# Attention probabilities normalised before their transposition, instead of the output after it

## The chip, the cores and the metric

The kernel runs on one core of a Trainium2 chip. The metric is device time in microseconds (us) of one execution. The core has five engines that run their own instruction streams and meet only at semaphores: TensorE (PE; its weight loads are listed apart as PEld), VectorE (DVE), ScalarE (ACT), GpSimd (POOL) and SyncE (SP), which here only starts transfers.

## What is computed

Two transformer-like layers on 1024 tokens of width 1024 in float32. The change touches only the two attentions of the second layer. Of the reference that is:

```python
# dilated_window_attention: three patterns, each softmax(q k^T / 8 + bias) v, merged by their
# denominators: one softmax over all positions, with a bias table per head
p = jnp.exp(s - m)
den = jnp.sum(p, axis=-1)
o = jnp.einsum('bnrhqk,bnkrhd->bnqrhd', p, vw) / den_q[..., None]
...
# latent_attention, per block of 128 queries
s = jnp.where((qpos[:, None] >= kpos[None, :])[None, None], s, -jnp.inf)
p = jax.nn.softmax(s, axis=-1)
return jnp.einsum('bhqk,bkhd->bqhd', p, v)
...
mixed = jnp.concatenate([o_a * jax.nn.silu(z_a), o_b * jax.nn.silu(z_b)], axis=-1)
```

So each attention output is divided by the sum of its exponentials and multiplied by a gate (`z_a`, `z_b`).

## The kernel before

The first layer and the projections of the second are large matrix products on PE. The attentions come late: stage A (the dilated one) fills about 2042 to 2177 us of the span, stage B (the latent one) about 2230 to 2387 us, with the latent projections in between.

Each stage has 32 **units**. A unit is a pair of heads (`j`, 0 to 3) and a block of 128 queries (`qb`); `at_unit(u)` takes the blocks of a pair in the order 0, 7, 1, 6, 2, 5, 3, 4. I call them positions 0 to 7 of a pair. A unit with block `qb` sees w = 128 (qb + 1) keys, so its width goes 128, 1024, 256, 896, 384, 768, 512, 640, and eight units make one period of the pattern. Its steps:

- `z(u)` on PE: scores of both heads into the PSUM tile `sm`, of which there is one.
- `scores(u, hh)` on DVE (L2918 in the profile): adds the bias or mask, writes `att_s` in SBUF (four places, by unit) and the row extremum.
- `exps(u, hh)` on ACT (L2269): exponential in place, with the row sum in `small`.
- `roots(u)` on DVE (L2926): the reciprocal of the two sums, 128x2.
- `turn(u)` on PE (L1693): 2 (qb + 1) transpositions of 128x128 out of `att_s`, four to a PSUM bank. Such a group of four is a chunk. Three banks are used in turn, so a chunk waits until the third chunk before it has been copied out.
- The chunks are copied to `att_pt` in SBUF, those with an even number by ACT (L2281), the odd ones by DVE (L2939).
- `output(u)` on PE: first two products that spread the inverse sums over the 64 columns of each head (L1703, into `at_share_place()`), then the probabilities times `v` (L1709, into `at_o_place()`). Both places are single, so `output(u)` waits for `at_o_taken` of unit u - 1.
- Gating on DVE: gate times output (L2951), then times the spread inverse sums (L2953), which raises `at_o_taken`.

The order on each engine is written out by hand. PE runs, unit after unit, `turn(u)`, `z(u+3)`, `output(u)`. DVE runs the odd copies of u, `scores(u+3, 0)`, `roots(u+2)`, `scores(u+3, 1)`, then the gating of u. ACT runs an even copy of u, `exps(u+2, 0)`, the other even copies, `exps(u+2, 1)`. Each stage begins with `z` and `scores` of units 0 to 2, the exponentials of units 0 and 1 and `roots` of units 0 and 1. Line numbers such as L1693 are those of this kernel.

POOL does little here. In stage A it splits late weights once (L878, L880, about 2078 to 2085 us), at the start of stage B again, and in stage B, whenever a pair of heads is finished (`at_o_taken` has reached a multiple of eight), it splits the gated tiles into a high and a low part (`split_mix`, L1083 and L1085).

Of the kernel before, what the change touches and what calls it, by code (L numbers as in the profile page):

```python
# [8 lines left out]
P = 128  # L9
# [3 lines left out]
HALF = 512  # L13
# [3 lines left out]
C = 64  # L17
# [18 lines left out]
ALU = mybir.AluOpType  # L36
# [112 lines left out]
def merge_adds(q):  # L149
# [18 lines left out]
    "rk_post1", "rk_chain", "rk_local", "rk_state", "rk_y", "rk_y_sb", "rk_yc", "rk_yc_sb", "rk_yc_sq", "rk_var",  # L168
    "rk_var_ln", "rk_rstd", "rk_g", "rk_y_done",
    "g_split", "h_split", "bias_p", "n2_sq", "n2_ss", "n2_q", "at_z", "at_o_taken", "at_o",  # L170
    "at_p", "at_pt", "at_root", "at_half_gated", "rot", "sines",
    "hn_sq", "hn_ss", "rot_used", "rope_mid", "hn_rt", "mix_high", "c_high",
    "out_t", "w_high", "root", "high", "x_turned", "tok_root", "x_scaled", "sc_done", "sg_var", "sg_root",
    "sb_e", "sb_p", "c_first", "silu", "g_raw", "g_high", "angles", "x_normed", "p_free0", "p_free1",
# [18 lines left out]
def hybrid_layers(nc, x, mix_norm_g, w_in, gate_b, sc_conv_w, sc_out, sb_out, rw_mu, rw_w0, rw_w2,  # L193
# [10 lines left out]
    with ExitStack() as ctx:  # L204
# [12 lines left out]
        ident = fixed("ident", [P, P])  # L217
# [190 lines left out]
        gp = ctx.enter_context(nc.psum_tensor("gp", [P, 2, T], F32))  # L408
# [171 lines left out]
        def at_unit(u):  # L580

            return u // 8 % 4, BLOCK_ORDER[u % 8]

        def at_place(u):

            return u % 4 if u < UNITS else (0, 3, 2, 1)[u % 4]
# [19 lines left out]

        def at_o_place():
            return gp[:, 1, HALF:HALF + P]

        def at_share_place():  # L610
            return gp[:, 1, HALF + P:HALF + 2 * P]

        def at_small(kind, u, hh=None):

            c = 96 + 8 * kind + 2 * (u % 4)
            return small[:, c:c + 2] if hh is None else small[:, c + hh:c + hh + 1]
# [482 lines left out]
        def _(pe):  # L1099
# [433 lines left out]
            for ch in range(1, NCH):  # L1533
                u, q = divmod(ch, 2)
# [144 lines left out]
            def attention(units, scores, s_buf, pt_buf, v, evicted):  # L1679

                def z(u):
                    if u >= 1:
                        pe.wait_ge(s["at_s"], 2 * u)
                    scores(*at_unit(u))

                def turn(u):
                    pe.wait_ge(s["at_p"], 2 * (u + 1))
                    for c, r in at_chunks(u):
                        if r >= 3:
                            pe.wait_ge(s[f"at_pt_copied{(r - 3) % 2}"], (r - 3) // 2 + 1)  # L1690
                        for n, b in enumerate(at_blocks(u, c)):
                            k, hh = divmod(b, 2)
                            mm = pe.transpose(bank(4 + r % 3)[:, P * n:P * n + P],  # L1693
                                              s_buf[:, at_place(u), hh, P * k:P * k + P], ident[:, :])
                        mm.then_inc(s["at_pt"], 1)

                def output(u):
                    if u >= 1:
                        pe.wait_ge(s["at_o_taken"], u)
                    j, qb = at_unit(u)  # L1700
                    pe.wait_ge(s["at_root"], u + 1)
                    for hh in range(2):
                        pe.matmul(at_share_place()[C * hh:C * hh + C, :], at_small(2, u, hh).to_broadcast([P, C]),  # L1703
                                  ident[:, :], start=True, stop=True, skip_group_check=True)
                    for c, r in at_chunks(u):
                        pe.wait_ge(s[f"at_pt_copied{r % 2}"], r // 2 + 1)
                        for b in at_blocks(u, c):
                            k, hh = divmod(b, 2)
                            mm = pe.matmul(at_o_place()[C * hh:C * hh + C, :],  # L1709
                                           v[:, k, C * (2 * j + hh):C * (2 * j + hh) + C], pt_buf[:, u % 2, b, :],  # L1710
                                           start=(k == 0), stop=(k == qb), skip_group_check=True)
                    mm.then_inc(s["at_o"], 1)

                for u in units[0:3]:
                    z(u)
                for parity in range(2):
                    pe.wait_ge(s[f"p_free{parity}"], frees_before(evicted))
                for u in units:
                    turn(u)
                    if u + 3 in units:  # L1720
                        z(u + 3)
                    output(u)
                pe.wait_ge(s["at_s"], 2 * (units[-1] + 1))
                pe.wait_ge(s["at_o_taken"], units[-1] + 1)
# [612 lines left out]
        def _(dve):  # L2337
# [103 lines left out]
            for m in range(PAIRS):  # L2441
                w = P * (m // 2 + 1)
# [468 lines left out]
            def attention(units, table_of, s_buf, pt_buf, gate, step, beside=lambda u: None):  # L2911

                def scores(u, hh):
                    w = P * (at_unit(u)[1] + 1)
                    dve.wait_ge(s["at_z"], 2 * u + hh + 1)
                    tab = table_of(u, hh)
                    a = 0 if u < UNITS else HALF - w // 2
                    dve.tensor_tensor_reduce(  # L2918
                        out=s_buf[:, at_place(u), hh, 0:w],
                        in0=sm[:, 2 * hh:2 * hh + 2, :].rearrange("p a b -> p (a b)")[:, a:a + w],  # L2920
                        in1=tab[:, T - w:T], scale=1.0, scalar=3e38, op0=ALU.add, op1=ALU.min,
                        accum_out=at_small(0, u, hh)).then_inc(s["at_s"], 1)

                def roots(u):
                    dve.wait_ge(s["at_p"], 2 * (u + 1))
                    dve.reciprocal(at_small(2, u), at_small(1, u)).then_inc(s["at_root"], 1)  # L2926

                for u in units[0:3]:
                    for hh in range(2):
                        scores(u, hh)  # L2930
                    beside(u)
                for u in units[0:2]:
                    roots(u)
                for u in units:
                    for c, r in at_chunks(u):
                        if r % 2:
                            b = at_blocks(u, c)
                            dve.wait_ge(s["at_pt"], r + 1)
                            dve.tensor_copy(pt_buf[:, u % 2, b[0]:b[0] + len(b), :],  # L2939
                                            bank(4 + r % 3)[:, 0:P * len(b)].rearrange("p (b q) -> p b q", q=P)) \  # L2940
                                .then_inc(s["at_pt_copied1"], 1)
                    if u + 3 in units:
                        scores(u + 3, 0)
                    if u + 2 in units:
                        roots(u + 2)
                    if u + 3 in units:
                        scores(u + 3, 1)
                    dve.wait_ge(s["at_o"], u + 1)
                    j, qb = at_unit(u)
                    z = gate[:, j, P * qb:P * qb + P]  # L2950
                    dve.tensor_tensor(z, z, at_o_place()[:, ::step], ALU.mult).then_inc(s["at_half_gated"], 1)  # L2951
                    dve.wait_ge(s["at_half_gated"], u + 1)
                    dve.tensor_tensor(z, z, at_share_place()[:, ::step], ALU.mult).then_inc(s["at_o_taken"], 1)  # L2953

            def bias_table(u, hh):
                j = at_unit(u)[0]
# [135 lines left out]
```

## Time and profile before

| | us |
|---|---|
| median of 3 runs | 2491.04 (2487.88 to 2491.86) |
| the profiled execution | 2491.14 |
| its span | 2489.4 |
| PE busy | 2407.7 (97%) |
| DVE busy | 1100.2 (44%) |
| ACT busy | 712.3 (29%) |
| POOL busy | 1016.8 (41%) |
| TensorE clock granted, share of full speed | 0.99 |

The profile is of one execution. Its span leaves out 1.7 us of the time. An engine's busy share over the span says little about one stage; the two attentions are 11% of the span and are read by themselves. PE's clock has two levels, 1.2 and 2.4 GHz, shown as 0.5 and 1.0.

### The profile page before, as it was taken

What the parts mean: (1) busy time and instruction counts of PE and PEld (TensorE: products, weight loads), DVE (VectorE), ACT (ScalarE), POOL (GpSimd) and SP (SyncE); (2) the same over time, 40 slices, a digit from 0 to 9 for tenths busy, and PEclk for the clock granted to TensorE, in tenths of its full rate; (3) what the DMA queues carried; (4) which work ended last, traced back from release to release, by engine and by line L of the source; (5) the groups of instructions that cost most, each with busy time, mean ns of one, the idle gap of its engine ahead of it and who ended that gap; (6) DMA issues with size and microseconds to landing.
All of it is one profiled execution on the core that took longest, in us unless ns stands there. A gap on an engine that the chain in (4) does not pass through costs nothing.

```text
span 2489.4 us, 36188 instructions
## 1 busy us (share of the span) xinstructions
PE 2407.7 (97%) x15614; PEld 1906.9 (77%) x15614; DVE 1100.2 (44%) x1352; ACT 712.3 (29%) x1096; POOL 1016.8 (41%) x677
## 2 busy tenths in 40 slices
PE   7999999999999989999999999999999999989999
PEld 6888777777779868878888887888677876656677
DVE  5140113223186355676676664334333216655521
ACT  4101122232222122254344431012322015564411
POOL 4323323323223368577777763444622310002221
PEclk9999999999999999999999999999999999999999
DMA  5111322222210146423222225221113121000014
GB/s 195 50 44 44 97 80 77 85 68 81 67 31 4 46 145 210 136 68 93 85 76 82 88 97 182 102 86 59 49 36 110 43 68 39 1 24 12 1 60 127
DMA packets 208248, 189.82 MB, mean 76 GB/s; under 512 B 16714, under 2 KB 186929, under 8 KB 207834
## 3 DMA queue, kind: packets, MB, share of 16 engines
q1 hardware_dynamic: 208090, 187.51, 24.2%
q8 instruction: 124, 2.03, 0.3%
q14 instruction: 34, 0.28, 0.0%
HBM read 141.31 MB, written 45.13 MB: 75 GB/s over the span
## 4 chain that ended last, share of the span: by engine, by line
PE 89%; DVE 6%; ACT 2%; POOL 1%; issue 1%; DMA 0%; SPq 0%; DVEq 0%; POOLq 0%; ACTq 0%
PE gp L1113 14%; PE gp L1115 13%; PE gp L1114 13%; PE sm L1598 3%; PE sm L1599 3%; PE sm L1600 3%; PE gp L1598 3%; PE gp L1599 3%; PE gp L1600 3%; PE gp L1693 2%; PE gp L1709 2%; PE sm L1809 2%; PE gp L1627 2%; PE sm L1628 2%; PE sm L1627 2%; PE sm L1629 2%
## 5 line engine op out<-in xcount | busy, mean ns | idle before, releaser
L1113 PE MATMUL gp<-h_hi,w_hi 128*128 128x512 f32 x1264 | 508.4, 402 | 1.3 <-ACT k_sb L1921 1.3
L878 POOL CAST w_hi<-w_raw 128x1024 fp32r<-128x1024 f32 (+1 forms) x121 | 130.8, 1081 | 918.3 <-PE gp L1115 537.6
L1115 PE MATMUL gp<-h_hi,w_lo 128*128 128x512 f32 x1264 | 493.8, 391 | 0.0
L1114 PE MATMUL gp<-h_lo,w_hi 128*128 128x512 f32 x1264 | 493.5, 390 | 0.0
L880 POOL TENSOR_TENSOR w_lo<-w_raw,w_hi 128x1024 fp32r<-128x1024 f32 (+1 forms) x129 | 341.9, 2650 | 10.3 <-ACT w_hi L2049 0.5
L1113 PEld LDWEIGHTS gp<-h_hi,w_hi 128*128 128x128 f32 x1264 | 237.8, 188 | 70.8 <-issue 23.7
L1114 PEld LDWEIGHTS gp<-h_lo,w_hi 128*128 128x128 f32 x1264 | 238.0, 188 | 51.2 <-issue 4.3
L1115 PEld LDWEIGHTS gp<-h_hi,w_lo 128*128 128x128 f32 x1264 | 237.8, 188 | 50.9
L2445 DVE TENSOR_TENSOR_SCAN sb_run<-sb_keep,ones_row 128x128 f32<-128x128 f32 (+7 forms) x32 | 77.1, 2449 | 318.1 <-POOL sb_keep L925 318.1
L1046 POOL TENSOR_TENSOR w_lo<-w_sum,w_hi 128x512 fp32r<-128x512 f32 x66 | 96.4, 1461 | 45.8 <-ACT w_hi L2108 45.8
L2269 ACT ACTIVATE att_s<-att_s,small 128x1024 f32<-128x1024 f32 (+7 forms) x128 | 98.7, 773 | 10.6 <-DVE small L2918 10.2
L1693 PE MATMUL gp<-ident,att_s 128*128 128x128 f32 x576 | 79.4, 281 | 10.8 <-DVE att_pt L2939 10.8
L2281 ACT COPY att_pt<-gp 128x512 f32<-128x512 f32 (+1 forms) x80 | 44.9, 562 | 130.9 <-PE gp L1693 130.9
L1933 ACT ACTIVATE gate_out<-gp,col 128x1024 f32<-128x1024 f32 x32 | 35.7, 1116 | 157.4 <-PE gp L1115 157.4
L1693 PEld LDWEIGHTS gp<-ident,att_s 128*128 128x128 f32 x576 | 61.7, 141 | 24.5 <-DVE att_pt L2939 12.7
L1598 PE MATMUL gp<-x_hi_T,w_hi 128*128 128x512 f32 x176 | 69.7, 396 | 5.9 <-DVE up_u L2762 5.2
L925 POOL TENSOR_SCALAR_AFFINE_SELECT sb_sig<-sb_sig 128x256 f32<-128x256 f32 x16 | 6.5, 407 | 167.5 <-ACT sb_keep L1945 167.5
L998 POOL TENSOR_TENSOR merged<-merged,gated 128x1024 f32<-128x1024 f32 x24 | 64.8, 2698 | 18.8 <-DVE gated L2634 16.4
L1627 PE MATMUL gp<-g_hi,w_hi 128*128 128x512 f32 x176 | 69.4, 395 | 3.0 <-DVE g_lo L2807 3.0
L2191 ACT CAST g_hi<-g_stage 128x1024 fp32r<-128x1024 f32 x22 | 23.0, 1051 | 169.5 <-DMA g_stage<-g_spill 124.2
L2918 DVE CUSTOM_DVE_ANT_0 att_s<-sm,ones_row 128x128 f32<-128x128 f32 (+7 forms) x64 | 47.6, 748 | 50.5 <-PE sm L1815 50.5
L1600 PE MATMUL gp<-x_hi_T,w_lo 128*128 128x512 f32 x176 | 69.3, 394 | 0.0
(528 smaller groups left out, 5232.3 us busy)
## 6 DMA issues: line engine op xcount, KB each, us to landing
w_raw<-in_w_in SPq DMA_DIRECT2D x79, 512.0 KB, 4.4
gates_spill<-gate_out SPq DMA_DIRECT2D x32, 512.0 KB, 3.1
gate_in<-gates_spill SPq DMA_DIRECT2D x30, 512.0 KB, 4.3
w_raw<-in_w_up SPq DMA_DIRECT2D x22, 512.0 KB, 5.0
up_raw<-in_w_up SPq DMA_DIRECT2D x22, 512.0 KB, 5.0
g_spill<-hid SPq DMA_DIRECT2D x22, 512.0 KB, 2.6
g_stage<-g_spill SPq DMA_DIRECT2D x22, 512.0 KB, 4.4
w_raw<-in_w_down SPq DMA_DIRECT2D x22, 512.0 KB, 3.6
```

Of the source, the lines that this page charges most:

```text
L878: pool.tensor_copy(w_hi[:, t % 2, 0:n], w_raw[:, t % 2, 0:n]).then_inc(s["w_high"], 1)
L880: pool.tensor_tensor(w_lo[:, t % 2, 0:n], w_raw[:, t % 2, 0:n], w_hi[:, t % 2, 0:n].bitcast(F32), ALU.subtract).then_inc(s["w_split"], 1)
L1046: pool.tensor_tensor(lo, w_quad(n), hi.bitcast(F32), ALU.subtract).then_inc(s["up_low"], 1)
L1113: pe.matmul(o, wh, hi[:, k0 + k, c], start=(k == 0), stop=False)
L1114: pe.matmul(o, wh, lo[:, low[k] if low else k0 + k, c], start=False, stop=False)
L1115: mm = pe.matmul(o, wl, hi[:, k0 + k, c], start=False, stop=(k == n - 1))
L1598: pe.matmul(o, wh, xh[:, :], start=(i < 4 and j == 0), stop=False, skip_group_check=True)
L1599: pe.matmul(o, wh, xl[:, :], start=False, stop=False, skip_group_check=True)
L1600: mm = pe.matmul(o, wl, xh[:, :], start=False, stop=(j == 3), skip_group_check=True)
L1627: pe.matmul(o, wh, hi[:, cols], start=(k == 0), stop=False)
L1693: mm = pe.transpose(bank(4 + r % 3)[:, P * n:P * n + P], s_buf[:, at_place(u), hh, P * k:P * k + P], ident[:, :])
L2269: act.activation(s_buf[:, at_place(u), hh, 0:w], s_buf[:, at_place(u), hh, 0:w], ACT.Exp, scale=-1.0, bias=at_small(0, u, hh), accum_out=a ...
```

## The change

The reciprocal is now applied to the probabilities in SBUF, before the transposition. DVE multiplies both heads' rows of `att_s` in place by the inverse sum (`even(u)`), PE's `turn(u)` waits for that instead of for the exponentials, the spreading products on PE are gone, and of the two gating products one is left. `even(u+2)` stands after `scores(u+3, 1)` and ahead of the gating of u; at the start of a stage `even(0)` and `even(1)` follow their reciprocals.

```diff
                 def turn(u):
-                    pe.wait_ge(s["at_p"], 2 * (u + 1))
+                    pe.wait_ge(s["at_even"], 2 * (u + 1))
...
                     j, qb = at_unit(u)
-                    pe.wait_ge(s["at_root"], u + 1)
-                    for hh in range(2):
-                        pe.matmul(at_share_place()[C * hh:C * hh + C, :], at_small(2, u, hh).to_broadcast([P, C]),
-                                  ident[:, :], start=True, stop=True, skip_group_check=True)
...
+                def even(u):
+                    dve.wait_ge(s["at_root"], u + 1)
+                    w = P * (at_unit(u)[1] + 1)
+                    for hh in range(2):
+                        row = s_buf[:, at_place(u), hh, 0:w]
+                        dve.tensor_scalar(row, row, at_small(2, u, hh), None, ALU.mult).then_inc(s["at_even"], 1)
+
...
                 for u in units[0:2]:
                     roots(u)
+                    even(u)
...
                     if u + 3 in units:
                         scores(u + 3, 1)
+                    if u + 2 in units:
+                        even(u + 2)
                     dve.wait_ge(s["at_o"], u + 1)
...
-                    dve.tensor_tensor(z, z, at_o_place()[:, ::step], ALU.mult).then_inc(s["at_half_gated"], 1)
-                    dve.wait_ge(s["at_half_gated"], u + 1)
-                    dve.tensor_tensor(z, z, at_share_place()[:, ::step], ALU.mult).then_inc(s["at_o_taken"], 1)
+                    dve.tensor_tensor(z, z, at_o_place()[:, ::step], ALU.mult).then_inc(s["at_o_taken"], 1)
```

On DVE, in unit 0 of stage A (the gating of unit 0 and the two copies of unit 1 that follow it), the kernel before has, with line L2918 for `scores`, whose second instruction reads out the accumulator:

```order
L2918 ISA att_s,small<-sm,w_raw 128x896 [waits at_z]
L2918 ISA small 128x1
L2951 TENSOR_TENSOR z_a<-z_a,gp 128x128 [waits at_o]
L2953 TENSOR_TENSOR z_a<-z_a,gp 128x128 [waits at_half_gated]
L2939 COPY att_pt<-gp 128x512 [waits at_pt] x2
```

The changed kernel has there, with `even(2)`, 256 wide, in between (its line numbers differ):

```order
L2911 ISA att_s,small<-sm,w_raw 128x896 [waits at_z]
L2911 ISA small 128x1
L2926 TENSOR_SCALAR att_s<-att_s,small 128x256 [waits at_root]
L2926 TENSOR_SCALAR att_s<-att_s,small 128x256
L2954 TENSOR_TENSOR z_a<-z_a,gp 128x128 [waits at_o]
L2940 COPY att_pt<-gp 128x512 [waits at_pt] x2
```

Two multiplications have come in ahead of the gating and of the copies, and one gating product has gone.

On PE, in unit 1 of stage A, from the fourth chunk of `turn(1)` to the start of `output(1)`, before:

```order
L1693 MATMUL gp<-ident,att_s 128x128 [waits at_pt_copied1]
L1693 MATMUL gp<-ident,att_s 128x128 x3
L1733 MATMUL sm<-k_261,q_260 128x384 [waits at_s]
L1733 MATMUL sm<-k_261,q_260 128x384
L1703 MATMUL gp<-ident,small 64x128 [waits at_root,at_o_taken]
L1703 MATMUL gp<-ident,small 64x128
L1709 MATMUL gp<-att_pt,v_262 64x128 [waits at_pt_copied1]
```

And now:

```order
L1690 MATMUL gp<-ident,att_s 128x128 [waits at_pt_copied1]
L1690 MATMUL gp<-ident,att_s 128x128 x3
L1726 MATMUL sm<-k_261,q_260 128x384 [waits at_s]
L1726 MATMUL sm<-k_261,q_260 128x384
L1702 MATMUL gp<-att_pt,v_262 64x128 [waits at_pt_copied1,at_o_taken]
```

The two spreading products are gone, and the wait for `at_o_taken` has moved to the first product with `v`.

## Rows read from the trace of the kernel before

**Rows 1.** The page: busy time of the engines, and the chain that ended last.

```profile
PE 2407.7 (97%) x15614; PEld 1906.9 (77%) x15614; DVE 1100.2 (44%) x1352; ACT 712.3 (29%) x1096; POOL 1016.8 (41%) x677
PE 89%; DVE 6%; ACT 2%; POOL 1%; issue 1%; DMA 0%; SPq 0%; DVEq 0%; POOLq 0%; ACTq 0%
```

**Rows 2.** Stretches: length, PE, PEld, DVE, ACT, POOL busy (count), PEclk, DMA share, GB/s.

```profile
2047.50:2177.00 129.50, 118.48 (x1173) 83.74 (x1173) 87.52 (x261) 71.24 (x167) 6.01 (x4) 0.99 0.11 27
2231.00:2391.70 160.70, 150.17 (x1508) 103.75 (x1509) 91.69 (x268) 71.09 (x168) 31.36 (x20) 0.97 0.07 19
2079.50:2111.20 31.70, 29.87 (x302) 21.11 (x300) 21.81 (x67) 17.72 (x42) 4.95 (x3) 1.00 0.17 44
2276.00:2313.00 37.00, 35.37 (x378) 24.75 (x376) 21.63 (x67) 17.72 (x42) 6.73 (x4) 1.00 0.01 2
```

**Rows 3.** PE's waits, stage A then B: us in total, times, longest.

```profile
PE sm L1733 <- DVE small L2918: 6.0, 5, 4.6
PE gp L1693 <- DVE att_pt L2939: 5.3, 4, 1.3
...
PE gp L1693 <- DVE att_pt L2939: 5.4, 4, 1.4
```

**Rows 4.** Timeline, positions 0 to 1, stage A: start, us, engine, line, idle before.

```profile
2086.72 0.44 PE L1703 MATMUL gp<-ident,small 128*64 128x128 f32 x4
...
2086.99 0.39 PE L1709 MATMUL gp<-att_pt,v 128*64 128x128 f32 x4
...
2087.31 1.53 PE L1693 MATMUL gp<-ident,att_s 128*128 128x128 f32 x12
...
2088.91 0.28 DVE L2951 TENSOR_TENSOR z_a<-z_a,gp 128x128 f32<-128x128 f32 x1
...
2089.23 0.29 DVE L2953 TENSOR_TENSOR z_a<-z_a,gp 128x128 f32<-128x128 f32 x1
2089.43 1.28 DVE L2939 COPY att_pt<-gp 128x512 f32<-128x512 f32 x2
...
2090.17 0.66 PE L1693 MATMUL gp<-ident,att_s 128*128 128x128 f32 x4 [1.33 <-DVE att_pt L2939]
```

**Rows 5.** DVE lines (min/median/max ns), and the timeline of one, alone and beside POOL.

```profile
L2918 DVE CUSTOM_DVE_ANT_0 att_s<-sm,ones_row x64: 269/748/1225, 2231.1 to 2377.8; 128x128 f32<-128x128 f32 x8, 128x1024 f32<-128x1024 f32 x8, 128x256 f32<-128x256 f32 x8, 128x896 f32<-128x896 f32 x8
...
L2354 DVE TENSOR_SCALAR x_tok<-x_tok,small x8: 739/744/2824, 13.0 to 24.6; 128x1024 f32<-128x1024 f32 x8
...
22.64 2.73 DVE L2354 TENSOR_SCALAR x_tok<-x_tok,small 128x1024 f32<-128x1024 f32 x4
...
17.12 2.66 POOL L880 TENSOR_TENSOR w_lo<-w_raw,w_hi 128x1024 fp32r<-128x1024 f32 x1
17.51 2.82 DVE L2354 TENSOR_SCALAR x_tok<-x_tok,small 128x1024 f32<-128x1024 f32 x1
```

**Rows 6.** Timeline, start of a unit's `z` and `turn` in stage A's first units.

```profile
2051.59 0.69 PE L1693 MATMUL gp<-ident,att_s 128*128 128x128 f32 x2
...
2052.52 2.62 PE L1733 MATMUL sm<-k,q 64*128 64x512 f32 x8 [0.24 <-DVE small L2918]
```

**Rows 7.** Timeline of POOL in stage B, behind a finished pair of heads.

```profile
2281.10 1.04 POOL L1083 CAST mix_hi<-z_a 128x1024 fp32r<-128x1024 f32 x1 [32.10 <-DVE z_b L2953]
2282.22 2.36 POOL L1085 TENSOR_TENSOR mix_lo<-z_a,mix_hi 128x1024 fp32r<-128x1024 f32 x1
```

**Rows 8.** Timeline, two POOL instructions in a row with a DVE instruction between.

```profile
1801.95 5.75 POOL L1019 TENSOR_TENSOR cos_t<-cos_t,end_sq 128x1024 f32<-128x1024 f32 x2
1802.24 3.20 DVE L2852 SCALAR_TENSOR_TENSOR c_kv<-c_kv,col,nrt 128x1024 f32<-128x1024 f32 x1 [2.57 <-ACT nrt L2230]
```

**Rows 9.** Timeline of PE just behind stage B.

```profile
2394.07 0.50 PE L1113 MATMUL gp<-mix_hi,w_hi 128*128 128x512 f32 x1 [1.92 <-POOL mix_lo L1085]
...
2395.94 0.63 PE L1114 MATMUL gp<-mix_lo,w_hi 128*128 128x512 f32 x1
...
2398.93 0.44 PE L1115 MATMUL gp<-mix_hi,w_lo 128*128 128x512 f32 x1
```

More of the change, by code:

```diff
@@ L170 @@
     "g_split", "h_split", "bias_p", "n2_sq", "n2_ss", "n2_q", "at_z", "at_o_taken", "at_o",
-    "at_p", "at_pt", "at_root", "at_half_gated", "rot", "sines",
+    "at_p", "at_pt", "at_root", "at_even", "rot", "sines",
     "hn_sq", "hn_ss", "rot_used", "rope_mid", "hn_rt", "mix_high", "c_high",
@@ L608, in at_o_place @@
             return gp[:, 1, HALF:HALF + P]
-        def at_share_place():
-            return gp[:, 1, HALF + P:HALF + 2 * P]
         def at_small(kind, u, hh=None):
```

## Prediction, made before the changed kernel was run

> **What bounds the kernel now.** I read the page first: PE is busy 97% of the span and the chain that ended last runs through PE for 89% [rows 1]. So work taken from PE counts unless PE then waits for something else. The busy times by stretch tell more. In the two attentions PE is busy 118.5 of 129.5 us and 150.2 of 160.7 us, DVE 87.5 and 91.7 us [rows 2]. One period of eight units takes about 31.7 us in stage A and 37.1 us in stage B, DVE being busy 21.8 and 21.6 us of it. DVE has room in the sum, but PE's waits are all for DVE: once a period, 1.3 us for a copy of a chunk in either stage, and in stage A 6.0 us for the scores, 4.6 of it at the start [rows 3]. The timeline shows the first of these [rows 4]: `turn` of position 1 has 16 blocks, 12 go through from 2087.31, and the last four wait 1.33 us, until 2090.17, for DVE's copy begun at 2089.43. This copy stands in DVE's queue behind the gating of the unit before. The change inserts its new work in exactly that queue.
>
> **What PE is spared.** The four matmuls of L1703 (two heads, each in two passes) start at 2086.72 and the product with `v` at 2086.99 [rows 4], so they hold PE 0.27 us. 64 units give 17.3 us, 2.16 us a period. That is the most the change can bring on PE. The load of weights goes with it and was beside other work.
>
> **What DVE gets.** The nearest row is L2354, a TENSOR_SCALAR in place on float32 in SBUF with its factor read from `small`, just as `even` is: 744 ns for 1024 columns, and four in a row take 2.73 us [rows 5], which is (2.73 - 0.74) / 3 = 0.66 us from start to start. `scores` (L2918) takes 269 ns at 128 columns and 1225 at 1024, 1.07 ns a column; 744 ns for 1024 can only be two columns in that time, 0.53 us, which leaves 0.13 us fixed (an estimate from these rows). A pair of `even` of width w then costs w x 1.04 ns + 0.26 us: 0.39 us at 128, 0.53 at 256, 0.79 at 512, 0.93 at 640, 1.33 at 1024. A period has 4608 columns a head: 4.8 + 8 x 0.26 = 6.9 us. The gating loses 0.32 us (2088.91 to 2089.23) [rows 4], 2.6 us a period. DVE grows by 4.3 us to 26.1 us of some 31 us. It is not the bound in sum, only by its place in the order.
>
> **What of it lands on the path.** I laid the four queues of one period out, with the starts of the timeline for the old instructions, the pair costs above, and 0.27 us less for each unit on PE. Against the 2.16 us:
> - Position 1, fourth chunk: `even` of 256 columns comes in (+0.53) and one gating goes (-0.32), PE is there 0.27 earlier. The wait of 1.33 us becomes 1.80. +0.47 us.
> - Position 5: `output` waits for its second chunk's copy, which is behind `even` of 512 columns (0.79). +0.31 us in A, about 0 in B, where `z` is longer.
> - Position 7: `z` and then `output` wait for DVE, which has the scores of a 1024 wide unit and `even` of 128 columns ahead. +0.6 us in A, +0.4 in B.
> - Position 0: `z` waited for scores already, 0.4 us, and this shrinks as PE comes later. -0.3 us in A, -0.2 in B.
> The rest of `even` is hidden: DVE waited for `z` or `output` there anyway. (There DVE has slack until `z` or `output` is done, or the copy comes before PE asks for it.) The sum is +1.1 us in A and +0.7 us in B, so a period gains 1.0 us in A and 1.5 us in B. Three whole periods of each: -7.6 us. The first units and the last two of a stage come out near zero: `turn(0)` now waits for `even(0)` behind three units' scores, at 2053.0 instead of 2051.59, and `z(3)`, which began at 2052.52 [rows 6], is behind it. That costs 0.7 us in A and 0.8 in B, one gating less at the end and the other early units give it back. PE and DVE alone: about **-7.5 us**. With `even` a quarter dearer it would be -4.5; at no fixed cost at all -12.
>
> **What else it meets.** The same row has a maximum of 2824 ns: the instruction at 17.51 took 2.82 us while a POOL TENSOR_TENSOR ran from 17.12 to 19.78 [rows 5]. So `even` is held while such a POOL instruction runs. In stage B POOL works for some 7 us behind each pair of heads, 1.04 and 2.36 us twice over, 0.06 us behind the gating that releases it [rows 7]. By my layout the `even` of 256 columns arrives 3.4 us after that gating, at the end of the first 2.36 us instruction, and it is the one on the path of the fourth chunk. From both sides: if both heads slip through between two POOL instructions it is 0.15 us, if it must wait for all four it is 3.5 us. I take 1.2 us, one CAST between the two heads, because where two POOL instructions stood in a row a waiting DVE instruction came in after the first (3.20 us for it, against 5.75 us for the two) [rows 8]. Three places in B, and one like it in A at about 2080 us, make **+4.7 us**, between +0.4 and +10. The Trainium skill, "SBUF — State Buffer", Who interferes with whom, says that the port pair VectorE shares with GpSimd is an exclusive lock, held for a whole instruction. The trace agrees, with 2.82 against 0.74 us.
>
> **The clock.** Behind stage B PE waited 1.92 us, and 1.5 us later its matmuls took 0.63 us, and 0.44 only from 2398.93 on: the clock had fallen from 2.4 to 1.2 GHz [rows 9]. Waits of 1.33 us inside the stages led to no fall (granted 1.00 over a whole period) [rows 2]. The new wait, 1.80 us and with POOL up to 3, is nearer to the first than to the second. The slow matmuls stand from 2395.6 to 2398.9, so one fall costs at most half of 3.4 us, 1.7. In the start of A PE already runs slow and will be idle another 1.4 us; I count +1.3 us there. For the eight waits, two at +0.2 us to three at +0.5 us each is a guess; I put **+2 us** in all with the start, between 0 and +14.
>
> **Sum.** -7.5 + 4.7 + 2 = -0.8 us. Against the profiled execution (2491.14, span 2489.4) that is 2490.3; its time is within 0.1 us of the median 2491.04. Since the two costs are the less certain parts and one may fail to appear, I name 2489.5. A difference under 0.2%, 5 us, is what a measurement of this kernel cannot tell from none.
>
> **Rivals.**
> 1. Even trade, as summed: 2486 to 2495 us. For it: the single waits of [rows 3] are for DVE, and the unit's 0.27 us is met by more DVE work ahead of PE's waits. Against: two of its terms are guesses. 0.50.
> 2. The gain stands, POOL and the clock don't matter: `even` slips between POOL's instructions and waits of 1.8 us keep the clock. Then 2491.0 - 7.5 = 2483.5, between 2480 and 2486. For it: PE at 1.00 over whole periods, and POOL is idle in nearly all of stage A. 0.28.
> 3. The clock falls behind the lengthened wait at position 1. It decides if the wait of 1.80 us works on the clock as that of 1.92 us did. If it falls at all eight: -7.5 + 4.7 + 1.3 + 8 x 1.6 = +11.3, so 2502; if at five, 2497.5. For it: [rows 9]. Against: the calculated wait is 1.80, not 1.92. 0.17.
> 4. The multiplication does not run at two columns a cycle here, so a pair costs w / 480 + 0.26. That is 4.8 us more DVE work a period, of which I'd put 3 us on the path: 8 x 3 = +24, 2514 us. Row L2354 speaks against it, having the same operands. 0.03.
> 5. The change doesn't reach what it says: `turn` waits for `at_even` where the exponentials were long done, so each `turn` starts later. In my layout `even(u+1)` always ends ahead of the gating of u - 1, which `output(u)` needs anyway, so this would show at the first units only: +2 us. 0.02, counted in 1.
>
> The range from 2482 to 2501 leaves out rival 4, the worst of 3 and the best of 2. **Chances:** faster by over 0.2%: 0.30. Within: 0.49. Slower: 0.21.
>
> **What the profile of the changed kernel would show.** L1703 gone and PE's instructions fewer by 256, with PE's busy time down some 17 us. The new DVE line 128 times, with 0.74 us at 1024 columns and 0.27 at 128. A period of 30.6 us in A and 35.6 us in B where POOL is idle. PE's wait for the copy (L1693's line, four times a stage) at 1.8 us. In stage B single `even` instructions of 256 columns at over 1 us, right behind a finished pair. The clock at 1.00 in the periods. I'd be wrong if periods come out near 29.6 us in A (then DVE hid nearly everything), above 31.7 us (then DVE bounds the stage), or if the time moves outside the two attentions.

## The result, and the profile after

The changed kernel takes **2497.66 us** (median; 2493.85 to 2501.53), the kernel before in the same rounds 2490.94 (2487.88 to 2493.53). The ratio is 1.0028, 95% interval 1.0020 to 1.0036: slower by about 7 us, where 2489.5 was forecast. The time lies inside the predicted range, on the side that was given the smallest chance. A fourteenth execution of the changed kernel ran at a granted clock of 0.748 over its whole span and took 3025.82 us; it is left out of these thirteen.

The profile is of an execution of 2501.53 us, the longest of these. Its busy times and its chain, where before it was [rows 1]:

```profile
span 2499.8 us, 35740 instructions
PE 2403.3 (96%) x15358; PEld 1900.6 (76%) x15358; DVE 1139.2 (46%) x1416; ACT 712.2 (28%) x1096; POOL 1017.6 (41%) x677
PE 89%; DVE 7%; POOL 1%; ACT 1%; issue 1%; DMA 0%; SPq 0%; DVEq 0%; POOLq 0%; ACTq 0%
```

PE has the 256 instructions fewer, but its busy time fell by 4.4 us only, where 256 times 0.068 us, 17 us, had been taken out. So other matmuls have become longer. The stretches show which (columns as in [rows 2]): stage A and stage B, then two periods of stage A that hold the same instructions.

```profile
2047.50:2179.10 131.60, 115.87 (x1044) 79.97 (x1045) 103.75 (x292) 70.60 (x165) 5.99 (x4) 0.95 0.10 24
2232.50:2401.50 169.00, 150.79 (x1390) 102.64 (x1389) 113.01 (x300) 71.12 (x168) 32.10 (x19) 0.92 0.06 17
2105.99:2138.43 32.44, 29.78 (x267) 20.81 (x265) 25.88 (x75) 17.72 (x42) 0.00 (x0) 0.95 0.17 46
2138.43:2169.25 30.82, 28.16 (x267) 19.35 (x265) 25.70 (x75) 17.73 (x42) 0.00 (x0) 1.00 0.00 1
```

The granted clock is 0.95 and 0.92 over the stages, against 0.99 and 0.97 in [rows 2]. The last two rows are the lesson in small: same work, DVE and ACT busy for the same time, PE 1.62 us longer in the first, clock 0.95 against 1.00, and the period longer by the same 1.62 us. A period of the kernel before takes 31.66 us there (two take 63.32 us, from 2090.17 to 2153.49): the second of these is 0.8 us shorter, the first 0.8 us longer.

The starts of the first `z` of each stage (2042.26 and 2229.90 before, 2041.23 and 2232.02 now) split the 10.4 us by which this execution's span is longer. Up to stage A it is 1.0 us ahead, from there to the first `z` of stage B it takes 3.2 us more, and from there to the end 8.3 us more. What follows the last product of stage B takes 0.3 us less than before. So it all comes from the two attentions.

PE's waits in stage A, then in stage B (us in total, times, longest), to be laid beside [rows 3]:

```profile
PE sm L1726 <- DVE small L2911: 6.7, 5, 4.6
PE gp L1690 <- DVE att_pt L2940: 6.6, 4, 1.8
PE gp L1702 <- DVE att_pt L2940: 3.7, 5, 1.5
PE gp L1690 <- DVE att_s L2926: 1.5, 1, 1.5
...
PE gp L1690 <- DVE att_pt L2940: 10.0, 4, 2.6
```

The wait for the copy of the fourth chunk at position 1 has gone from 1.33 to 1.76 us in three of the four periods of stage A (1.31 us in the first), and from 1.36 to 2.35 us in the first and 2.55 us in the others of stage B. What follows on PE is in the timeline: first the two periods of stage A, the start of `turn`'s last four blocks and then the product with `v`; below them the same in stage B.

```profile
2092.66 0.66 PE L1690 MATMUL gp<-ident,att_s 128*128 128x128 f32 x4 [1.76 <-DVE att_pt L2940]
2094.09 1.97 PE L1702 MATMUL gp<-att_pt,v 128*64 128x128 f32 x32
...
2123.49 0.65 PE L1690 MATMUL gp<-ident,att_s 128*128 128x128 f32 x4 [1.76 <-DVE att_pt L2940]
2124.92 3.50 PE L1702 MATMUL gp<-att_pt,v 128*64 128x128 f32 x32
...
2330.09 1.12 PE L1690 MATMUL gp<-ident,att_s 128*128 128x128 f32 x4 [2.55 <-DVE att_pt L2940]
2333.67 3.46 PE L1702 MATMUL gp<-att_pt,v_b 128*64 128x128 f32 x32
```

The 32 matmuls of this product take 1.97 us at the full clock. Behind the three waits of 1.76 us they took 1.97 us twice and 3.50 us once, where PE had fallen from 2.4 to 1.2 GHz. In this execution I find six such places inside the stages, near 2084, 2125, 2255, 2292, 2330 and 2371 us. The second and the last four follow the wait at position 1; the first follows a wait of 1.47 us of `output`. "Inside a stage" leaves out its start: before `turn(0)` has run, PE waits 4.56 us (A) and 2.5 us (B) for the first scores, and the clock falls there in the kernel before and in every other kernel of this study. Other than that, the kernel before has no fall inside its stages.

Why the wait is so much longer in stage B is seen on DVE and POOL, behind a finished pair of heads:

```profile
2287.30 2.37 POOL L1082 TENSOR_TENSOR mix_lo<-z_a,mix_hi 128x1024 fp32r<-128x1024 f32 x1
2289.61 1.16 POOL L1080 CAST mix_hi<-z_b 128x1024 fp32r<-128x1024 f32 x1
...
2289.53 1.39 DVE L2926 TENSOR_SCALAR att_s<-att_s,small 128x256 f32<-128x256 f32 x2
2290.84 0.28 DVE L2954 TENSOR_TENSOR z_b<-z_b,gp 128x128 f32<-128x128 f32 x1
```

The two multiplications of 256 columns take 0.61 us where POOL is idle and 1.39 us here. One goes through, POOL's CAST runs until 2290.77, then comes the other. DVE meets POOL at two more places: in the first pair of heads of stage B, where POOL splits weights from 2244 to 2252 us, the multiplications of 1024 and of 256 columns take 2.19 and 1.19 us (1.41 and 0.61 alone), and in stage A those of 128 columns near 2082 us take 1.37 us (0.48 alone).

### The profile page after: what moved, and what is told of

It is laid out like the page before. It is cut to its first block, busy times and chain, and to the rows that moved or that the text cites. A ratio compares the mean times of both kernels' runs of the same rounds, so it can differ in the third digit from the quotient of the medians.

```text
span 2499.8 us, 35740 instructions
## 1 busy us (share of the span) xinstructions
PE 2403.3 (96%) x15358; PEld 1900.6 (76%) x15358; DVE 1139.2 (46%) x1416; ACT 712.2 (28%) x1096; POOL 1017.6 (41%) x677
## 4 chain that ended last, share of the span: by engine, by line
PE 89%; DVE 7%; POOL 1%; ACT 1%; issue 1%; DMA 0%; SPq 0%; DVEq 0%; POOLq 0%; ACTq 0%
PE gp L1110 14%; PE gp L1112 13%; PE gp L1111 13%; PE sm L1597 3%; PE sm L1595 3%; PE sm L1596 3%; PE gp L1702 3%; PE gp L1595 3%; PE gp L1597 3%; PE gp L1596 3%; PE gp L1690 2%; PE sm L1802 2%; PE sm L1626 2%; PE sm L1625 2%; PE sm L1624 2%; PE gp L1624 2%
## 5 line engine op out<-in xcount | busy, mean ns | idle before, releaser
L877 POOL TENSOR_TENSOR w_lo<-w_raw,w_hi 128x1024 fp32r<-128x1024 f32 (+1 forms) x129 | 341.9, 2650 | 10.3 <-ACT w_hi L2042 0.5
L1596 PE MATMUL gp<-x_lo_T,w_hi 128*128 128x512 f32 x176 | 69.3, 394 | 0.0
```

What stands on the lines that cost most here:

```text
L877: pool.tensor_tensor(w_lo[:, t % 2, 0:n], w_raw[:, t % 2, 0:n], w_hi[:, t % 2, 0:n].bitcast(F32), ALU.subtract).then_inc(s["w_split"], 1)
L1596: pe.matmul(o, wh, xl[:, :], start=False, stop=False, skip_group_check=True)
```

## The experiments

All ratios are to the kernel before, run in the same rounds on the same chip, with their 95% intervals. "Period" is the time from a place in one unit to the same place eight units on, in the profiled execution; "fall" is a place where PE's matmuls go on at half clock inside a stage, its start left out.

### What the spared work is worth: no division, and both

`e1_no_division` takes `even` out again and leaves the division out altogether:

```diff
-                    pe.wait_ge(s["at_even"], 2 * (u + 1))
+                    pe.wait_ge(s["at_p"], 2 * (u + 1))
...
-                    if u + 2 in units:
-                        even(u + 2)
```

> The changed kernel without its multiplications on DVE: no spreading on PE, no division at all, one gating product (the output is not the reference's, the division by the sums is left out). It measures what PE is spared and nothing else. All theories: 64 x 0.27 = 17.3 us less than before, minus little: the wait for the fourth chunk at position 1 goes from 1.33 to about 1.28 us (PE 0.27 earlier, one gating less). 2474 us, clock as before (0.99). If it stays above 2483 the spared PE time is given back by some other wait, and the first term of the sum was wrong.

Measured: 2479.46 us, ratio 0.9956 (0.9942 to 0.9970). The periods are 30.03 and 35.44 us, against 31.66 and 37.07 before. So the removed work is worth 1.63 us a period, not 2.16. It came out 5 us above what was expected. PE arrives earlier and meets more of DVE's work: its waits for `scores` grew by 0.9 us in each stage, and `output` now waits 1.2 us (A) and 0.7 us (B) for copies, where it waited for none. The shorter waits for the fourth chunk give 0.8 us back; the rest of the 5 us is not accounted for.

`e2_both` is the other end, the kernel before with `even` put in: spreading and both gating products stay, and the result is divided twice.

```diff
+                    pe.wait_ge(s["at_root"], u + 1)
+                    for hh in range(2):
+                        pe.matmul(at_share_place()[C * hh:C * hh + C, :], at_small(2, u, hh).to_broadcast([P, C]),
+                                  ident[:, :], start=True, stop=True, skip_group_check=True)
...
-                    dve.tensor_tensor(z, z, at_o_place()[:, ::step], ALU.mult).then_inc(s["at_o_taken"], 1)
+                    dve.tensor_tensor(z, z, at_o_place()[:, ::step], ALU.mult).then_inc(s["at_half_gated"], 1)
+                    dve.wait_ge(s["at_half_gated"], u + 1)
+                    dve.tensor_tensor(z, z, at_share_place()[:, ::step], ALU.mult).then_inc(s["at_o_taken"], 1)
```

> The kernel before with the multiplications added on DVE and turn waiting for them; spreading and both gatings stay (rows are divided by their sum twice). It measures the DVE part alone. By the layout: +0.53 us at position 1, +0.3 at position 5, +0.5 at position 7, some 1.3 us a period, 10 us; start of the stages 2.5 us, POOL 3 us: 2506 us. If the clock falls as often as in the changed kernel another 8 us: 2514 us. If DVE's additions were simply in the way in full (6.9 us a period) 2546 us.

Measured: 2512.26 us, ratio 1.0087 (1.0072 to 1.0103). `even` alone costs 21.9 us (the kernel before took 2490.36 in these rounds). The wait at position 1 is 1.5 to 1.9 us in A and up to 2.9 us in B, and there are five falls. The reading "with the clock" came closest, 2 us below. From these two, `even` where it stands costs 18.2 us (2497.66 - 2479.46) in the changed kernel. What part of it is clock they don't say.

### The clock: fillers in the wait

`e3_filled` leaves the order of the changed kernel as it is and gives PE twelve useless products at position 1, into the bank that the third chunk will fill next. They end before that chunk's transpositions, and PE then waits for DVE's copy less long or not at all. The copy itself comes no earlier.

```diff
+                        if c == 2 and at_unit(u)[1] == 7:
+                            for _ in range(FILL):
+                                pe.matmul(bank(4 + r % 3)[:, 0:P], ident[:, :], ident[:, :],
+                                          start=True, stop=True, skip_group_check=True)
```

> The changed kernel, and in turn of position 1, ahead of the third chunk's transpositions, 12 products of the identity with itself into the bank that these transpositions then overwrite: about 1.3 us of PE work that stands in time in which PE waited 1.8 us for DVE's copy. Clock theory (the falls behind this wait cost the 7 us): the clock stays at 1.0 at these eight places, 5 to 6 falls of up to 1.7 us go, 2489 us. POOL or queue theory (the waits themselves cost it): no change, 2497 us, or a little more.

Measured with `FILL = 12`: 2494.34 us, ratio 1.0016 (1.0007 to 1.0024), no falls inside the stages. The fillers held PE 2.6 us, more than the 1.76 us of the wait in A, so they gave back a part of what they saved. Neither number was hit. `e5_filled6` is the same with `FILL = 6`:

> As e3 with 6 products in place of 12. In e3 the twelve took 2.6 us, more than the wait, and the clean period of stage A was 31.5 us in place of 30.8. Six take 1.3 us and fit in the wait of 1.76 us. Clock theory: no fall behind position 1 and no path cost, so 8 x 0.7 us less than e3 and 10 us less than the worst run of the changed kernel: 2489 us. Queue or POOL theory: as the changed kernel, 2497 us.

Measured: **2491.24 us**, ratio 1.0004 (0.9995 to 1.0013), from 2490.38 to 2493.28 in eleven executions. Its timeline at the place of the first rows above:

```profile
2091.40 0.66 PE L1695 MATMUL gp<-ident,att_s 128*128 128x128 f32 x4 [0.41 <-DVE att_pt L2945]
...
2092.83 1.97 PE L1707 MATMUL gp<-att_pt,v 128*64 128x128 f32 x32
```

and a period and the two stages, as stretches:

```profile
2092.83:2123.65 30.82, 29.50 (x278) 20.69 (x277) 25.69 (x74) 17.73 (x43) 0.00 (x0) 1.00 0.17 49
2047.50:2178.00 130.50, 119.85 (x1100) 84.17 (x1101) 103.45 (x293) 72.26 (x166) 5.98 (x4) 0.97 0.09 24
2231.50:2392.00 160.50, 149.15 (x1429) 101.99 (x1425) 112.90 (x296) 70.23 (x165) 32.86 (x20) 0.96 0.07 19
```

The six fillers take 1.34 us of the wait and leave 0.41 us. PE does 1.34 us more a period and the period is 30.82 us, exactly that of the undisturbed one above. There is no fall inside either stage. PE works more, DVE as much as in the changed kernel, and 6.4 us are gone (2497.66 - 2491.24). That is the price of the falls, shown by taking them away with DVE's order untouched. The two profiled executions agree on the size. Length times what the clock lacks to 1.00 is 131.6 x 0.05 + 169.0 x 0.08 = 20.1 us in the stages of the changed kernel and 130.5 x 0.03 + 160.5 x 0.04 = 10.3 us here; that is 9.8 us less, and the executions lie 10.4 us apart (2501.53 and 2491.11). One of the six falls, that near 2084 us, is not at position 1. Here `output` waits 1.44 us at that place and no fall follows; that the fillers did this is not shown.

`e11_before_filled` puts four fillers into the kernel before, as a control:

> The kernel before with four such products (0.9 us in the wait of 1.33 us). A control: the clock does not fall there before, so both theories expect no change, 2490.9 us. If it gets faster by more than 2 us, the products do something else than keep the clock.

Measured: 2491.15 us, ratio 1.0005 (0.9996 to 1.0013): no difference that can be told from none. Where there was no fall, fillers gained nothing.

### POOL: its work moved away

`e4_mix_late` splits the gated tiles at the end of stage B and not during it. Only the stages are to be read, since the end is then late (2513.21 us, one execution).

```diff
-                pool.wait_ge(s["at_o_taken"], UNITS + NB * (j + 1))
+                pool.wait_ge(s["at_o_taken"], 2 * UNITS)
```

> The changed kernel with POOL's splitting of the gated tiles put off for all pairs until the last unit of stage B, so that POOL is idle during the multiplications; the end of the kernel gets longer by about 20 us for it, so only stage B is to be read. POOL theory: the wait for the fourth chunk in pairs 1 to 3 of stage B goes from 2.56 to 1.76 us as in stage A, and every multiplication of 256 columns takes 0.35 us. Clock theory: with the shorter wait the clock falls less often, the period comes to 35.6 us or, with a fall, 37 us. If POOL is not the cause the wait stays at 2.56 us.

Measured, in stage B: the pair of multiplications takes 0.61 us again and the wait is 1.77 us, as in stage A.

```profile
2284.02 0.61 DVE L2926 TENSOR_SCALAR att_s<-att_s,small 128x256 f32<-128x256 f32 x2
...
2285.48 0.65 PE L1690 MATMUL gp<-ident,att_s 128*128 128x128 f32 x4 [1.77 <-DVE att_pt L2940]
...
2287.72 3.33 PE L1702 MATMUL gp<-att_pt,v_b 128*64 128x128 f32 x32
```

So POOL is what makes 0.8 us of the wait in B. Three falls stay; the two whole periods of 37.58 us have one each. A wait of 1.77 us can be enough for a fall, and POOL only adds to it. It is not always enough: stage A of this kernel is that of the changed kernel, it has waits of 1.75 us as well, and no fall follows any of them. These rows are the third pair of heads, where the 32 matmuls took 3.50 us in the changed kernel:

```profile
2120.82 0.66 PE L1690 MATMUL gp<-ident,att_s 128*128 128x128 f32 x4 [1.75 <-DVE att_pt L2940]
...
2122.25 1.97 PE L1702 MATMUL gp<-att_pt,v 128*64 128x128 f32 x32
```

### The place of `even` in DVE's order

`e7_one_moved` moves one `even` in eight, that of position 2 (256 columns), from ahead of position 1's copies to between them. Number and size of all instructions are those of the changed kernel.

```diff
+                            if u % 8 == 1 and c == 0:
+                                even(u + 1)
...
-                    if u + 2 in units:
+                    if u + 2 in units and u % 8:
                         even(u + 2)
```

> The changed kernel with one multiplication in eight moved: that of position 2 (256 columns) goes behind the first copy of position 1, which it was ahead of. Only the wait for the fourth chunk is touched. Clock theory: this wait goes from 1.76 and 2.56 back to 1.28 us, the falls behind it with it: 8 x 0.5 + 3 x 0.9 + 5 to 7 falls of 1.5 us, 2483 us. If the clock has no part, 6.7 us less: 2491 us. If the other positions are the cause, within 2 us of 2497.

Measured: 2486.64 us, ratio 0.9985 (0.9976 to 0.9994), 11.0 us below the changed kernel. The waits at position 1 are 1.2 us in both stages, there are no falls behind them, and the clean period of B is 36.01 us. It lies between two of the readings. If the clock's part is the 6.4 us of `e5_filled6`, the rest, 4.6 us, is the wait itself (an estimate). The waits at position 1 are 7.0 us shorter in the profiled execution (6.6 to 4.6 us in A, 10.0 to 5.0 in B); in stage B 1.0 us of it comes back in `output`'s waits and 0.8 us in that of `turn(0)`.

`e6_even_late` moves all of them: `even(u+1)` follows the odd copies of u, ahead of `scores(u+3)`.

```diff
+                    if u + 1 in units:
+                        even(u + 1)
                     if u + 3 in units:
                         scores(u + 3, 0)
...
-                    if u + 2 in units:
-                        even(u + 2)
```

> The changed kernel with even(u+1) behind the odd copies of unit u, ahead of scores(u+3), in place of even(u+2) ahead of the gating of u. DVE does the same work; it falls into time in which DVE waits for z. If the place in the queue is the cause, the waits at position 1 shrink to 1.3 us and at 5 and 7 to 0.2, the clock stays, the periods come to 30.2 (A) and 35.5 us (B) as in the kernel without the division, and with POOL's part and the later turn(0) 2484 us. If DVE's extra work as such is the cause, no change: 2497 us.

Measured: 2481.57 us, ratio 0.9965 (0.9952 to 0.9977). Periods 30.11 and 35.44 us. What was left were two waits at the start of a stage, where `turn(0)` waits 1.5 and 2.5 us for `even(0)` behind three units' `scores`. `e8_late_early0` does the first reciprocal and `even(0)` before the third unit's `scores`:

```diff
+                    if u == units[1]:
+                        roots(units[0])
+                        even(units[0])
+                roots(units[1])
```

> As e6, with reciprocal and multiplication of unit 0 ahead of the scores of unit 2, so that turn(0) no longer waits for them behind three units' scores (1.5 and 1.7 us, and slow clock). If these starts cost what the layout says, 1 to 3 us less than e6; if the wait for z(2)'s scores takes its place, the same as e6.

Measured: **2478.74 us**, ratio 0.9953 (0.9941 to 0.9966), the best of this study and some 12 us below the kernel before. It can't be told from the kernel without any division (2479.46) within their intervals: all of the 128 multiplications are hidden. POOL still holds them up in stage B (2.02 us for the pair of 256 columns behind a finished pair of heads, more than the 1.39 of the changed kernel), but there they stand behind the copies, and the period is 35.43 us all the same. Its stretches (a period, then the stages) have DVE as busy as the changed kernel's:

```profile
2090.96:2121.07 30.11, 28.00 (x266) 19.37 (x264) 25.86 (x74) 17.72 (x43) 0.00 (x0) 1.00 0.17 49
2047.50:2168.00 120.50, 107.85 (x1000) 74.04 (x1002) 102.52 (x288) 71.08 (x168) 6.05 (x4) 0.99 0.13 32
2231.50:2382.00 150.50, 139.75 (x1372) 94.84 (x1365) 115.11 (x293) 70.24 (x164) 34.47 (x19) 0.97 0.07 20
```

and its waits for the copy (stage A, then stage B) are a little shorter than those of the kernel before:

```profile
PE gp L1690 <- DVE att_pt L2941: 4.9, 4, 1.2
...
PE gp L1690 <- DVE att_pt L2941: 4.8, 4, 1.2
```

### The wait alone, in the kernel before

`e9_wait_before` puts only position 2's `even` into the kernel before, four times a stage (those rows are divided twice). `e10_wait_before_filled` adds six fillers to it. If the lengthened wait makes the falls, they should come without any other part of the change.

```diff
+                    if u % 8 == 2:
+                        pe.wait_ge(s["at_even"], 2 * (u // 8 + 1))
...
+                    if u + 2 in units and u % 8 == 0:
+                        even(u + 2)
```

> The kernel before, with spreading and both gatings, and one multiplication of 256 columns added a period, that of position 2, ahead of the gating of position 0 (that unit's rows are divided by their sum twice). It lengthens the wait at position 1 by 0.53 us, to 1.86 us, and in pairs 1 to 3 of stage B by some 0.9 us more through POOL. Counted as DVE time alone: 8 x 0.53 + 3 x 0.9 = 6.9 us, 2497.7 us. Clock theory: falls behind these waits as in the changed kernel, another 5 to 8 us: 2504 us, and clock 0.987.

> As e9 with the six products ahead of the third chunk. Clock theory: 2497.7 us, clock 0.99. Otherwise the same as e9.

Measured: 2510.51 us, ratio 1.0080 (1.0067 to 1.0093), and 2508.24 us, ratio 1.0071 (1.0058 to 1.0083). Both were missed, by 6.5 and 10.5 us, and the sum in these expectations was wrong for stage B. Their intervals overlap, so the times do not show that the fillers gained anything here. In stage A they came out as expected: the wait is 1.86 us, a period without a fall 32.18 (+0.52), one with a fall 33.84, and with fillers both are 32.18. A fall costs 1.66 us there. The two periods of `e9_wait_before` in stage A:

```profile
2091.16 0.66 PE L1695 MATMUL gp<-ident,att_s 128*128 128x128 f32 x4 [1.86 <-DVE att_pt L2948]
2092.86 1.92 PE L1711 MATMUL gp<-att_pt,v 128*64 128x128 f32 x32
...
2123.34 0.66 PE L1695 MATMUL gp<-ident,att_s 128*128 128x128 f32 x4 [1.85 <-DVE att_pt L2948]
2125.15 3.48 PE L1711 MATMUL gp<-att_pt,v 128*64 128x128 f32 x32
```

In stage B the wait is up to 4 us, and DVE and POOL show why:

```profile
2290.09 1.03 POOL L1083 CAST mix_hi<-z_b 128x1024 fp32r<-128x1024 f32 x1
...
2291.01 2.70 DVE L2935 TENSOR_SCALAR att_s<-att_s,small 128x256 f32<-128x256 f32 x2
2291.20 2.36 POOL L1085 TENSOR_TENSOR mix_lo<-z_b,mix_hi 128x1024 fp32r<-128x1024 f32 x1
...
2294.89 0.66 PE L1695 MATMUL gp<-ident,att_s 128*128 128x128 f32 x4 [3.97 <-DVE att_pt L2948]
```

The first of the two starts about where POOL's CAST ends; the second must let POOL's next instruction go first, and here that is the TENSOR_TENSOR of 2.36 us, until 2293.56. In the changed kernel the pair arrives one POOL instruction earlier, and the one that comes between is the CAST. The same rule, a price of 2.1 us (2.70 - 0.61) or 0.8 us (1.39 - 0.61), depending on when the pair arrives. Six fillers don't cover a wait of 4 us, and the falls stay in stage B.

## Why the prediction was wrong

**The direction.** The sum was -7.5 + 4.7 + 2 = -0.8 us. The time came out at +6.7. Step by step:

- *What PE is spared*: 256 instructions gone, as counted. The 2.16 us a period is the most, and 1.63 us of it arrives even with DVE spared too (`e1_no_division`).
- *What DVE gets*: right. 0.61 us for a pair of 256 (0.53 was estimated) and 1.41 for 1024 (1.33). DVE is busy 25.7 us in a clean period of A (26.1). That `even` is not the bound in sum but by its place is shown by `e8_late_early0`, which hides all of it.
- *Position 1*: 1.80 us predicted, 1.76 measured. The clean period of A is 30.82 us for 30.6. In B it is 36.0 us for 35.6 (36.74 in `e5_filled6`, less 0.8 for POOL), so a period gains 0.84 and 1.12 us where I had 1.0 and 1.5, and six of them give 5.9 us for the 7.6. The start of stage A came out as laid out: counted from the stage's first `z`, `turn(0)` starts 1.38 us later than before (10.71 us for 9.33), for 1.41 predicted (2053.0 - 2051.59).
- *POOL*: the mechanism was the right one, one CAST between the two heads. The term was mis-sized: 0.8 us a place (2.56 against 1.77 us in `e4_mix_late`), where I took 1.2. The first period of A, which meets POOL too, is 0.76 us longer than the clean one (31.58 against 30.82 in `e5_filled6`). That makes 4 x 0.8 = 3.2 us for 4.7. The first pair of stage B, where POOL splits weights, was not among the four places. Its wait is 2.35 us; what of that is POOL's was not measured by itself.
- *The clock*: **this is the step that failed.** For the waits at position 1 it had two falls at 0.2 to three at 0.5 us, called a guess, some 0.7 us in all. Measured are 6.4 us (`e5_filled6`), which is four falls of 1.6 us, and six inside the stages of the profiled execution, which is the longest of the thirteen. The price of one fall stood in the prediction ("at most 1.7"), and rival 3 had the mechanism and this price: with five falls 2497.5 us, near the 2497.66 measured. So close a hit is luck, since its other terms were off. The sum went wrong in the price of a fall: 0.2 to 0.5 us, where the row allowed up to 1.7 and the runs show 1.6. A fall costs nothing or 1.6 us, so the term is their expected number times 1.6. Only two kinds of waits were in the trace, 1.33 us with no fall and 1.92 us with one [rows 9], and even the second was not the sure sign that I took it for. The same wait behind stage B, 1.89 to 1.94 us, stands in twelve of these kernels' profiles. A fall follows it in six of them (before, changed, `e1_no_division`, `e5_filled6`, `e7_one_moved`, `e10_wait_before_filled`) and none in the other six. The changed kernel and `e8_late_early0`:

```profile
2404.45 0.50 PE L1110 MATMUL gp<-mix_hi,w_hi 128*128 128x512 f32 x1 [1.89 <-POOL mix_lo L1082]
...
2405.39 0.63 PE L1110 MATMUL gp<-mix_hi,w_hi 128*128 128x512 f32 x1
...
2384.41 0.50 PE L1110 MATMUL gp<-mix_hi,w_hi 128*128 128x512 f32 x1 [1.89 <-POOL mix_lo L1082]
...
2385.21 0.40 PE L1110 MATMUL gp<-mix_hi,w_hi 128*128 128x512 f32 x1
```

An even chance for each of the eight waits, at 1.6 us, is 6.4 us (an estimate, made with hindsight).

Without the falls this change would have come out near the sum: 2491.24 us in `e5_filled6`, where the sum without the 0.7 us for position 1 is 2489.6. In part that is two errors that cancel: in B a period of `e5_filled6` gains 0.32 us (36.74 for 37.06), just the 0.3 of the sum, because both the gain (1.1 for 1.5) and POOL's price (0.8 for 1.2) were taken 0.4 too high. Of the sum's miss of 7.4 us (2497.66 - 2490.3), 5.7 are the clock term and 1.7 all the rest together. The named forecast, 2489.5, was 0.8 lower still, for one of the two costs failing to appear; both appeared. The ratio of `e5_filled6` to before is 1.0004 (0.9995 to 1.0013), so even then the kernel would not have been measurably faster. What the spreading products gave, the place of `even` took back, and the falls came on top.

**The signs that the prediction named.** It said that a granted clock of 1.00 in the periods would show it right; it was 0.95 in one period of A. PE's busy time was to fall by 17 us and fell by 4.4. It named "above 31.7 us" as the sign that DVE bounds the stage. A period of 32.44 us did come, but DVE is no busier in it than in the one of 30.82: the clock did it.

**What stays open.** Why one wait of 1.76 us is followed by a fall and the next is not. `e9_wait_before` has the same with 1.86 and 1.85 us, so the length of the wait alone doesn't decide. The number of falls also differs from one execution to the next: stage A of the changed kernel has two in its own profile and none in that of `e4_mix_late`, where it is the same. The times fit this. The changed kernel's lie 7.7 us apart, those of `e5_filled6` 2.9, and each execution of the changed kernel has a granted clock of its own: 0.986 in five of the thirteen, 2497.78 to 2501.53 us, and 0.989 in the fastest, 2493.85. Over a span of 2500 us, 0.003 of the clock is 7.5 us. Nor was it measured by itself what the slow start of stage A costs. Its `z(3)` takes 3.36 us instead of the 2.62 of [rows 6], which is 0.7 us for the 1.3 I had put there, and the products behind it are slower too. From the stage's first `z` to the product with `v` at position 1 it is 19.68 us, against 17.37 in `e1_no_division` and in `e8_late_early0`: 2.3 us for start and clock together, where I had 2.0.

## What to carry to other kernels

Work moved from PE to an engine with room in the sum pays only if it is not queued ahead of what PE waits for next. Here the same 128 instructions cost 18 us in one place of DVE's order and nothing in another. When an edit makes a single PE wait longer, ask for the clock separately: price the fall from a row where one is seen (here 1.6 us), and treat each wait as a yes or no with a chance. One row with a fall doesn't give that chance: the same wait fell in six profiles of twelve. If the order can't be changed, a few useless products inside the wait can be worth it (6.4 us for 48 of them), but more than the wait holds costs again (3.1 us for twice as many).

## What the runs showed of the hardware

- Inside the stages, no fall was seen behind waits of 1.36 us or less (the kernel before, `e1_no_division`, `e6_even_late`, `e8_late_early0`). Behind 1.44 and 1.52 us there was none (`e5_filled6`, `e2_both`), behind 1.47 us one, in a period with a POOL delay. Of 18 waits at position 1 of 1.71 to 1.89 us 8 had a fall behind them (the changed kernel, `e2_both`, `e4_mix_late`, `e9_wait_before`), of ten of 2.3 to 4.0 us 9 (the changed kernel, `e2_both`, `e9_wait_before`).
- DVE and POOL alternated where both had work in SBUF: of two TENSOR_SCALAR of 256 columns, 0.35 us each, the second waited for one whole POOL instruction and was then let in, before the next one of POOL. The price was therefore that of the POOL instruction that happened to be next (1.04 or 2.36 us), and an arrival 4.35 us behind the start of POOL's first instruction (`e9_wait_before`, 2286.66) instead of 3.34 us (the changed kernel, 2286.19) made a wait of 4.0 us out of 2.6. The Trainium skill, "SBUF — State Buffer", Who interferes with whom, calls the port pair that the two share an exclusive lock, held for the whole instruction, which these rows bear out.
- A product of 128x128 in float32 with 128 columns held PE 0.22 us here (1.34 us for six), and a transposition of the same size 0.11 us (a group of four takes 0.66 us, one of eight 1.09).
